# Two of four token blocks through all experts densely, two gathered in one VectorE stream

## The chip, the cores and the metric

One core of one Trainium2 chip runs the kernel. The metric is the device time of one execution in microseconds (us). Everything is float32.

## The reference

A decoder layer on 512 tokens of width 1024. `x = LayerNorm(alpha*x + mixer(x))`, then `out = LayerNorm(alpha*x + PEER(x))`. The mixer is a projection into 3584 columns, four heads of chunked retention and four heads of differential attention, and an output projection. PEER is a retrieval over 16384 experts of one neuron each. Per token and head (8 heads), two query halves are scored against 128 keys each; the best 16 of each half give 256 sums, of which the best 16 name experts, `expert = i*128 + j`, and a softmax over their scores gives the gates. Then

```
u = peer_u[idx]; h = gelu(sum_d x[d] * u[e, d])      # e = 128 picks per token
y = sum_e gate[e] * h[e] * peer_v[idx[e]]
```

One expert row of u or v is 4 KB.

## The kernel before

The program is written engine by engine with semaphores, each engine's instructions in a fixed order. Tokens go in four blocks of 128 (one per partition). Block 0 passes the whole mixer first (`project_0`, `out_0`), gets x1 and its queries, and its experts are then worked on beside the mixer of blocks 1 to 3. Those three share one weight pass (`project_1`), attend one after the other (`attend`, `mixed_out`), get x1 (`ln1(b)`, L1247) and their queries together (`query(1, ...)`, L729). Weights of 2 MB come through two or four slots on SP's queue (`load_w`).

Retrieval of two heads of one block (`retrieve`, L1258) is `best_keys`, `best_pairs` and `best_experts` on VectorE; it writes scores and indices, and ScalarE takes the Exp.

Block 0 gathers u rows and v rows one by one (L438): each indirect DMA brings one row per partition, 0.5 MB, into a ring of 8. VectorE multiplies a u row with x1 and sums it in one instruction (`dots`, L1039; the token block was copied to PSUM). Of the 128 v rows, 32 are scaled and summed on TensorE by diagonal matrices that ScalarE makes from the gates (`diagonals`, `add_rows`, L461), 96 are added into xs on VectorE (`sums`, L1052). `rows(n)` on VectorE takes n groups of four rows and is called in the gaps of the mixer's VectorE work.

Blocks 1 to 3 gather u and v of an expert together (L426), 1 MB per DMA, into 18 slots that cover most of the arena once the mixer is done. VectorE does the dot (L1060), ScalarE the Gelu in groups of four (L971), VectorE the product with the gate (L1067), ScalarE the diagonal (L979), TensorE two matmuls of 512 columns (`add_pairs`, L474). `join_sums` adds the residual and `finish` is the last LayerNorm, then SP stores the block. VectorE's order around all this is its program from L1356 on.

## Time and profile before

| | |
|---|---|
| median of 3 runs | 1658.43 us (1653.55 to 1658.89) |
| span of the profiled execution | 1633.5 us |
| time around the span (median less span) | 24.9 us |
| TensorE, VectorE, ScalarE, GpSimd busy | 78%, 71%, 16%, 38% |
| moved by DMA | 603 MB, mean 369 GB/s |

The profile is of one execution, from its first to its last instruction; the page gives no time of its own for what lies around that, so the runs' median stands beside it. A busy engine is one with an instruction in work, not one at its peak. "PEclk" is the clock granted to TensorE as a share of 2.4 GHz; the DMA share is the mean busy share of sixteen DMA engines, and can read a little above 1. An fp32 matmul appears as two instructions.

### The profile page before, as it was taken

The numbers are of one execution on the slowest core, as the hardware profiler recorded it, in microseconds if no ns is written. First come the engines' busy times: TensorE is split into PE (matmuls) and PEld (weight loads), VectorE is DVE, ScalarE is ACT, GpSimd is POOL, SyncE is SP. The second block draws the span as 40 slices with busy tenths as digits, with TensorE's granted clock in tenths as the row PEclk, the third lists the DMA queues.
The fourth block names the chain that finished last, engine by engine and source line by source line (L and its number), as shares of the span: only waits on it lengthen the run. The fifth ranks groups of instructions, "written<-read, shape, count | busy, mean of one in ns | idle before, by whom it ended". The sixth has DMA issues, their size and how long they took to land.

```text
span 1633.5 us, 11511 instructions
## 1 busy us (share of the span) xinstructions
PE 1276.5 (78%) x3448; PEld 618.1 (38%) x3448; DVE 1155.6 (71%) x2727; ACT 267.2 (16%) x754; POOL 625.2 (38%) x645
## 2 busy tenths in 40 slices
PE   7879979888646994586978687878777878787885
PEld 5465446433323562232323233333333333332332
DVE  1349999767798979987676767776767677764454
ACT  0110000121211111121212121212121212121111
POOL 0004344474445565543434343434342434343320
PEclk9989999999767997798888888989897989899899
DMA  9939798897759898999999999999999999999993
GB/s 339 390 140 353 280 344 312 319 409 274 263 189 335 319 373 329 410 422 421 422 421 421 422 422 421 422 421 422 421 422 421 422 421 422 421 422 421 421 422 127
DMA packets 125710, 603.44 MB, mean 369 GB/s; under 512 B 12624, under 2 KB 14928, under 8 KB 76368
## 3 DMA queue, kind: packets, MB, share of 16 engines
q0 software_dynamic: 92160, 536.91, 81.2%
q1 hardware_dynamic: 33488, 65.80, 11.0%
q8 instruction: 27, 0.44, 0.1%
q14 instruction: 35, 0.29, 0.1%
HBM read 600.57 MB, written 2.10 MB: 369 GB/s over the span
## 4 chain that ended last, share of the span: by engine, by line
DMA 38%; PE 31%; DVE 23%; issue 3%; POOL 2%; SPq 1%; ACT 1%; DVEq 0%; POOLq 0%
DMA arena<-uv,idx 37%; PE W L474 7%; PE W L509 7%; DVE arena L1060 5%; PE ACC L474 4%; DVE xs L1052 4%; PE W L744 3%; PE W L716 3%; PE ACC L461 2%; POOL arena L438 2%; PE W L515 2%; DVE arena L1039 1%; DMA arena<-w_in 1%; DVE cand L1301 1%; DVE cand L1303 1%
## 5 line engine op out<-in xcount | busy, mean ns | idle before, releaser
L474 PE MATMUL W<-arena,fdiag 128*128 128x512 f32 x1024 | 498.9, 648 | 170.1 <-ACT fdiag L979 170.1
L426 POOL DMA_INDIRECT arena<-uv,idx x384 | 367.5, 957 | 586.7 <-PE W L474 355.7
L1060 DVE SCALAR_TENSOR_TENSOR arena<-arena,X 128x1024 f32<-128x1024 f32 x256 | 309.2, 1219 | 200.8 <-DMA arena<-uv,idx 199.7
L438 POOL DMA_INDIRECT arena<-uv,idx x256 | 257.3, 1005 | 372.2 <-DVE idx L1311 125.1
L474 PEld LDWEIGHTS W<-arena,fdiag 128*128 128x128 f32 x1024 | 208.6, 208 | 459.7 <-issue 253.0
L474 PE MATMUL ACC<-arena,fdiag 128*128 128x512 f32 x512 | 254.9, 660 | 69.3 <-ACT fdiag L979 69.3
L1060 DVE SCALAR_TENSOR_TENSOR arena<-arena,W 128x1024 f32<-128x1024 f32 x128 | 154.8, 1219 | 95.8 <-DMA arena<-uv,idx 95.4
L474 PEld LDWEIGHTS ACC<-arena,fdiag 128*128 128x128 f32 x512 | 107.0, 213 | 217.2 <-issue 132.1
L979 ACT ACTIVATE fdiag<-ident,gate 128x128 f32<-128x128 f32 x384 | 123.3, 390 | 354.7 <-DVE gate L1067 351.0
L1039 DVE SCALAR_TENSOR_TENSOR arena<-arena,X 128x1024 f32<-128x1024 f32 x128 | 150.0, 1216 | 24.8 <-DMA arena<-uv,idx 24.3
L509 PE MATMUL W<-arena 128*128 128x512 f32 x320 | 143.7, 605 | 9.7 <-DMA arena<-w_in 9.0
L1052 DVE SCALAR_TENSOR_TENSOR xs<-arena,gate,xs 128x1024 f32<-128x1024 f32 x96 | 123.3, 1284 | 19.3 <-DMA arena<-uv,idx 11.1
L744 PE MATMUL W<-arena 128*128 128x128 f32 (+1 forms) x512 | 116.8, 391 | 1.4 <-ACT arena L912 1.4
L971 ACT ACTIVATE hid<-hid 128x4 f32<-128x4 f32 x96 | 19.7, 205 | 456.5 <-DVE arena L1060 456.5
L744 PEld LDWEIGHTS W<-arena 128*128 128x128 f32 x512 | 80.2, 198 | 36.2 <-ACT arena L912 2.2
L509 PEld LDWEIGHTS W<-arena 128*128 128x128 f32 x320 | 60.8, 194 | 81.9 <-issue 76.9
L515 PE MATMUL W<-arena 128*128 128x128 f32 (+1 forms) x256 | 58.9, 388 | 10.8 <-DVE arena L1157 9.4
L461 PE MATMUL ACC<-arena,fdiag 128*128 128x512 f32 x128 | 59.0, 615 | 4.2 <-DMA arena<-uv,idx 4.2
L515 PEld LDWEIGHTS W<-arena 128*128 128x128 f32 x256 | 39.0, 194 | 28.4 <-issue 11.8
L716 PE MATMUL W<-arena 128*128 128x512 f32 x96 | 43.8, 616 | 0.7 <-ACT arena L912 0.7
L461 PEld LDWEIGHTS ACC<-arena,fdiag 128*128 128x128 f32 x128 | 24.5, 197 | 36.0 <-issue 29.7
L716 PEld LDWEIGHTS W<-arena 128*128 128x128 f32 x96 | 18.7, 198 | 25.1 <-issue 23.2
(178 smaller groups left out, 824.7 us busy)
## 6 DMA issues: line engine op xcount, KB each, us to landing
arena<-w_in SPq DMA_DIRECT2D x13, 2048.0 KB, 13.8
arena<-peer_w_query SPq DMA_DIRECT2D x8, 2048.0 KB, 14.4
arena<-uv,idx POOLq DMA_INDIRECT x640, 25.4
arena<-w_out SPq DMA_DIRECT2D x4, 2048.0 KB, 14.9
arena<-w_in SPq DMA_DIRECT2D x4, 512.0 KB, 6.4
out<-xs SPq DMA_DIRECT2D x4, 512.0 KB, 8.1
arena<-xT SPq DMA_DIRECT2D x1, 1536.0 KB, 18.2
xs<-x SPq DMA_DIRECT2D x1, 1536.0 KB, 17.0
```

Source lines behind the costliest of these rows:

```text
L426: pool.indirect_dma_start(out=fused[slot], out_offset=None, in_=uv, in_offset=bass.IndirectOffsetOnAxis(ap=idx[:, E + n:E + n + 1], axis=0 ...
L438: pool.indirect_dma_start(out=ring[:, r, :], out_offset=None, in_=rows, in_offset=bass.IndirectOffsetOnAxis(ap=idx[:, e:e + 1], axis=0), e ...
L461: last = nc.tensor.matmul(ACC[:, half * HW:(half + 1) * HW], fdiag[:, e % ND, :], ring[:, r, half * HW:(half + 1) * HW], start=e == 0, sto ...
L474: last = nc.tensor.matmul(sum_of(b)[:, half * HW:(half + 1) * HW], fdiag[:, n % ND, :], fused[n % NS][:, D + half * HW:D + (half + 1) * HW ...
L509: last = nc.tensor.matmul(bank, actT[:, k, part * P:(part + 1) * P], wts[slot][:, k, :], start=(k == 0), stop=(k == KD - 1))
L515: last = nc.tensor.matmul(bank[:, at:at + n_tok], wts[slot][:, k, h * P:(h + 1) * P], actT[:, k, toks], start=(k == 0), stop=(k == KD - 1))
L716: last = nc.tensor.matmul(W[:, 2 + half, :], mixT[:, k, :], wts[slot][:, k, :], start=(k == 0), stop=(k == KD - 1))
L744: last = nc.tensor.matmul(dst, wts[slot][:, k, i * P:(i + 1) * P], actT[:, k, toks], start=(k == 0), stop=(k == KD - 1))
L979: nc.scalar.activation(fdiag[:, n % ND, :], ident[:], ACT.Copy, scale=gate[:, E + n:E + n + 1]).then_inc(pair_diag_ready, 1)
L1039: STT(out=ring[:, r, :], in0=ring[:, r, :], scalar=1.0, in1=X[:], op0=ALU.mult, op1=ALU.mult, accum_out=hid[:, e:e + 1]).then_inc(slot_use ...
L1052: STT(out=xs[:, 0, :], in0=ring[:, r, :], scalar=gate[:, e:e + 1], in1=xs[:, 0, :], op0=ALU.mult, op1=ALU.add).then_inc(slot_used[r], 1)
L1060: STT(out=fused[slot][:, 0:D], in0=fused[slot][:, 0:D], scalar=1.0, in1=token_of(b), op0=ALU.mult, op1=ALU.mult, accum_out=hid[:, E + n:E ...
```

## The change

Blocks 1 and 2 (`DENSE`, 256 tokens together) pass through all 16384 experts in 128 tiles of 128 experts. `up(n)` computes the hidden values of tile n, experts on partitions, from a transposed copy of u (`uT`, made on the host like the other layouts); `hidden(n)` takes the Gelu into one of 56 slots; `mask_hidden(n)` multiplies by the gates, which are zero for experts not picked; `add(n, d)` multiplies with 128 rows of v and accumulates in PSUM over all tiles. The gate matrix is made per token from its 128 picks: `hot_quads` writes two one-hot matrices (pick by i, weighted with the gate, and pick by j) for four tokens at a time, `quad` multiplies them on TensorE to 128 x 128 gates, `take_quad` copies those to a stage, and every 32 tokens a stage of 2 MB is written to an array `gd` in device memory. From there `load_g` reads the gates of 8 tiles at a time, 1 MB in pieces of 1 KB.

Blocks 0 and 3 (`GATHERED`) gather in one stream of 512 single rows through the ring of 8, in the order u and v of block 0, u and v of block 3. All dots and all sums are on VectorE; the dot reads x1 in SBUF. `rows(n)` now counts single rows. The diagonals, `add_rows`, `add_pairs` and the copies of x1 to PSUM are gone. GpSimd's first gather waits for all four query products instead of two. Blocks are stored in the order 0, 3, 1, 2.

```diff
+GATHERED = [0, 3]
+DENSE = [1, 2]
+ROWS = 2 * E * len(GATHERED)
+ND = len(DENSE)
+TD = ND * P
+NT = P
+NH = 56
 NS = 18
-EARLY, LATE = 6, 14
-FG = 4
-ND = 6
-QUARTER = E // 4
+UR = 4
+VR = 4
+LEAD = 8
+TAIL = 4
+QUADS = P // 4
+OH_RING = 4
+OH_BANKS = 5
+CHUNK = 32
+NC = TD // CHUNK
+PER_CHUNK = CHUNK // 4
+GT = 8
+UP_FIRST = NH - ND * QUADS // 4
...
+            def load_u(n):
+                if n >= UR:
+                    sp.wait_ge(u_ready, n - UR + 1)
+                elif n < 2:
+                    sp.wait_ge(diff_mixed, NB)
+                else:
+                    sp.wait_ge(mixer_ready, 2 * NB)
+                sp.dma_start(u_ring[n % UR], uT[n].rearrange("p (k e) -> p k e", k=KD)).then_inc(u_landed[n % UR], 16)
+            def load_v(n):
+                if n >= VR:
+                    sp.wait_ge(v_done, n - VR + 1)
+                sp.dma_start(v_ring[n % VR], uv[n * P:(n + 1) * P, D:2 * D]).then_inc(v_landed[n % VR], 16)
+            def load_g(g):
+                if g >= 2:
+                    sp.wait_ge(masked, GT * (g - 1))
+                src = gd[:, :, g * GT:(g + 1) * GT, :].rearrange("c j i t -> j c (i t)")
+                sp.dma_start(g_ring[g % 2], src).then_inc(g_landed[g % 2], 16)
...
+            for i in range(WIN + WOUT + 2):
                 load_w(1, i)
-            sp.wait_ge(x1_ready, NB)
+            for n in range(UR):
+                load_u(n)
+            for i in range(WIN + WOUT + 2, PER_WAVE):
+                load_w(1, i)
+            for n in range(UR, NH + UR):
+                load_u(n)
+            for i in range(2):
+                sp.wait_ge(spill_landed[i], 16 * (NC // 2))
+            load_g(0)
+            for n in range(VR):
+                load_v(n)
+            load_g(1)
+            sp.wait_ge(quad_ready, ND * QUADS)
...
+            for n in range(NT):
+                if n + VR < NT:
+                    load_v(n + VR)
+                if n + NH + UR < NT:
+                    load_u(n + NH + UR)
+                if n % GT == 4 and n // GT + 2 < NT // GT:
+                    load_g(n // GT + 2)
...
+            pool.wait_ge(query_ready, WQ)
+            for s in range(ROWS):
+                g, e = s // (2 * E), s % E
+                col = g * E + e
+                is_u = s // E % 2 == 0
+                if is_u and e % QUARTER == 0:
+                    pool.wait_ge(experts_ready, 4 * GATHERED[g] + e // QUARTER + 1)
+                if s >= RING:
+                    pool.wait_ge(row_used[s % RING], s // RING)
...
+            def up(n):
+                pe.wait_ge(u_landed[n % UR], 16 * (n // UR + 1))
+                if n >= 2:
+                    pe.wait_ge(h_ready, n - 1)
+                for k in range(KD):
+                    last = nc.tensor.matmul(h_bank(n), u_ring[n % UR][:, k, :], actT[:, k, P:P + TD],
+                                            start=(k == 0), stop=(k == KD - 1))
+                last.then_inc(u_ready, 1)
...
+            def quad(q):
+                pe.wait_ge(hot_ready, q + 1)
+                if q >= OH_BANKS:
+                    pe.wait_ge(quad_taken, q - OH_BANKS + 1)
+                bank = quad_bank(q)
+                for m in range(4):
+                    last = nc.tensor.matmul(bank[:, m * P:(m + 1) * P], b_hot[:, q % OH_RING, m, :],
+                                            a_hot[:, q % OH_RING, m, :], start=True, stop=True)
+                last.then_inc(quad_ready, 1)
+            def add(n, d):
+                for half in range(2):
+                    last = nc.tensor.matmul(sum_banks(d)[:, half, :], h_slot(n)[:, d * P:(d + 1) * P],
+                                            v_ring[n % VR][:, half * HW:(half + 1) * HW],
+                                            start=(n == 0), stop=(n == NT - 1))
+                return last
...
+            for b in WAVES[1]:
+                attend(b)
+                mixed_out(b)
             turn_x1(3, out_banks(0))
             query(1, WAVES[1])
-            for b in range(1, NB):
-                add_pairs(b)
+            pe.wait_ge(scores_stored, 4 + 3 * WQ)
+            for n in range(UP_FIRST):
+                up(n)
+            for d in range(ND):
+                turn_picks(d)
+                for q in range(d * QUADS, (d + 1) * QUADS):
+                    quad(q)
+                    if q % 4 == 3:
+                        up(UP_FIRST + q // 4)
+            pe.wait_ge(quad_taken, ND * QUADS)
+            for n in range(NT - TAIL):
+                pe.wait_ge(masked, n + 1)
+                pe.wait_ge(v_landed[n % VR], 16 * (n // VR + 1))
+                for d in range(ND):
+                    last = add(n, d)
+                last.then_inc(v_done, 1)
+                if n + NH < NT:
+                    up(n + NH)
+            pe.wait_ge(masked, NT)
+            for i in range(VR):
+                pe.wait_ge(v_landed[i], 16 * (NT // VR))
+            for d in range(ND):
+                for n in range(NT - TAIL, NT):
+                    last = add(n, d)
+                last.then_inc(acc_ready, 1)
...
+            def hidden(n):
+                act.wait_ge(u_ready, n + 1)
+                if n >= NH:
+                    act.wait_ge(v_done, n - NH + 1)
+                elif n >= 48:
+                    act.wait_ge(experts_ready, 12)
+                elif n >= 40:
+                    act.wait_ge(experts_ready, 8)
+                nc.scalar.activation(h_slot(n), h_bank(n), ACT.Gelu).then_inc(h_ready, 1)
+            def take_picks(d):
+                act.wait_ge(experts_ready, 4 * d + 8)
+                nc.scalar.activation(pk[d % 2][:, 2, :], pk[d % 2][:, 2, :], ACT.Exp).then_inc(pk_exp_ready, 1)
+                act.wait_ge(pk_turned, d + 1)
+                nc.scalar.activation(pT[d % 2], ACC[:, HW:HW + 3 * P].rearrange("p (c t) -> p c t", c=3),
+                                     ACT.Copy).then_inc(pT_ready, 1)
+            def take_quad(q):
+                c, at = divmod(q, PER_CHUNK)
+                act.wait_ge(quad_ready, q + 1)
+                if at == 0 and c >= 2:
+                    act.wait_ge(spill_landed[c % 2], 16 * (c // 2))
+                nc.scalar.activation(stage[c % 2][:, :, 4 * at:4 * at + 4],
+                                     quad_bank(q).rearrange("p (m i) -> p i m", m=4), ACT.Copy).then_inc(quad_taken, 1)
+                if at == PER_CHUNK - 1:
+                    act.wait_ge(quad_taken, q + 1)
+                    nc.scalar.dma_start(gd[c], stage[c % 2]).then_inc(spill_landed[c % 2], 16)
...
+            gate_exp(0)
+            for b in WAVES[1]:
+                attention(b)
+                take_mixed(b)
+                if b > 1:
+                    take_x1(b - 1, out_banks(1))
             take_x1(3, out_banks(0))
...
             query(1, WAVES[1])
...
+            for n in range(UP_FIRST):
+                hidden(n)
+            for d in range(ND):
+                take_picks(d)
+                for q in range(d * QUADS, (d + 1) * QUADS):
+                    take_quad(q)
+                    if q % 4 == 3:
+                        hidden(UP_FIRST + q // 4)
+            gathered_gelu(0)
+            for n in range(NH, NT):
+                hidden(n)
+                if n == NH + 18:
+                    gate_exp(1)
+                elif n == NH + 64:
+                    gathered_gelu(1)
...
+            def norm_picks(d):
+                dve.wait_ge(pk_exp_ready, d + 1)
+                g = pk[d % 2][:, 2, :].rearrange("p (h k) -> p h k", h=PH)
+                link(nc.vector.reduce_sum(gsum[:], g, AX.X))
+                link(nc.vector.reciprocal(gsum[:], gsum[:]))
+                TT(out=g, in0=g, in1=gsum[:].unsqueeze(2).to_broadcast([P, PH, TOPK]),
+                   op=ALU.mult).then_inc(pk_ready, 1)
+            def hot_quads(d):
+                dve.wait_ge(pT_ready, d + 1)
+                for q in range(d * QUADS, (d + 1) * QUADS):
+                    if q >= OH_RING:
+                        dve.wait_ge(quad_ready, q - OH_RING + 1)
+                    for m in range(4):
+                        t = 4 * (q % QUADS) + m
+                        TS(b_hot[:, q % OH_RING, m, :], iota_f[:], pT[d % 2][:, 1, t:t + 1], None, ALU.is_equal)
+                        last = TS(a_hot[:, q % OH_RING, m, :], iota_f[:], pT[d % 2][:, 0, t:t + 1],
+                                  pT[d % 2][:, 2, t:t + 1], ALU.is_equal, ALU.mult)
+                    last.then_inc(hot_ready, 1)
+            def mask_hidden(n):
+                g = n // GT
+                if n % GT == 0:
+                    dve.wait_ge(g_landed[g % 2], 16 * (g // 2 + 1))
+                dve.wait_ge(h_ready, n + 1)
+                h = h_slot(n).rearrange("p (c t) -> p c t", c=NC)
+                TT(out=h, in0=h, in1=g_ring[g % 2][:, :, n % GT * CHUNK:(n % GT + 1) * CHUNK],
+                   op=ALU.mult).then_inc(masked, 1)
...
-                    rows(2)
+                    rows(4)
                     swish_gate(n)
                 else:
-                    rows(1)
+                    rows(2)
...
-            rows(3)
+            rows(8)
             ln1(3)
...
+            rows(12)
+            for s in range(4):
+                retrieve(1, s)
+                rows(3)
+            best_keys(2, 0)
+            norm_picks(0)
+            best_pairs()
+            best_experts(2, 0)
+            hot_quads(0)
+            for s in range(1, 4):
+                retrieve(2, s)
+                rows(3)
+            norm_picks(1)
+            rows(E - taken[0])
+            hot_quads(1)
+            weigh(0)
+            for n in range(LEAD):
+                mask_hidden(n)
+            for n in range(NT):
+                if n + LEAD < NT:
+                    mask_hidden(n + LEAD)
+                if 2 <= n < 14:
+                    s, stage_of = divmod(n - 2, 3)
+                    if stage_of == 0:
+                        best_keys(3, s)
+                    elif stage_of == 1:
                         best_pairs()
...
+                    else:
+                        best_experts(3, s)
+                if taken[0] == 3 * E and n < 66:
+                    pass
+                else:
+                    if n == 66:
+                        weigh(1)
+                    rows(min(4, 3 * E - taken[0]) if n < 66 else 3)
+                if n == 40:
+                    finish(0)
+                elif n == NT - 2:
+                    rows(ROWS - taken[0])
+                    finish(3)
+            for d in range(ND):
+                join_sums(d)
+                finish(DENSE[d])
...
```

## Rows read from the trace of the kernel before

**Rows 1.** Windows: us, busy (instructions) per engine, PEclk, DMA share, GB/s.

```profile
100.00:200.00 100.00, 96.57 (x445) 61.36 (x445) 88.08 (x273) 9.45 (x16) 30.11 (x32) 0.99 0.72 274
200.00:300.00 100.00, 90.37 (x345) 54.68 (x344) 96.94 (x253) 6.81 (x13) 48.73 (x52) 0.97 0.87 329
...
600.00:650.00 50.00, 28.37 (x118) 18.33 (x116) 45.37 (x86) 7.56 (x14) 27.56 (x26) 0.84 0.90 346
...
700.00:800.00 100.00, 78.53 (x159) 32.94 (x158) 75.21 (x184) 17.64 (x53) 38.19 (x40) 0.89 1.01 422
```

**Rows 2.** The page's chain that ended last, by line.

```profile
DMA arena<-uv,idx 37%; PE W L474 7%; PE W L509 7%; DVE arena L1060 5%; PE ACC L474 4%; DVE xs L1052 4%; PE W L744 3%; PE W L716 3%; PE ACC L461 2%; POOL arena L438 2%; PE W L515 2%; DVE arena L1039 1%; DMA arena<-w_in 1%; DVE cand L1301 1%; DVE cand L1303 1%
```

**Rows 3.** The chain in order of time: start us, us, what.

```profile
108.46 7.16 PE W L744 x64
...
172.48 6.87 PE W L509 x16
```

**Rows 4.** Timeline of VectorE, first MAX8 of two retrievals: start, us, what.

```profile
109.13 0.87 DVE L1269 MAX8 best_v<-arena 128x8 f32<-128x128 f32 x4 [14.47 <-ACT arena L935]
...
125.06 0.87 DVE L1269 MAX8 best_v<-arena 128x8 f32<-128x128 f32 x4
```

**Rows 5.** Timeline of VectorE, dots and sums; the landing of gathers, by tile.

```profile
141.06 1.21 DVE L1039 SCALAR_TENSOR_TENSOR arena<-arena,X 128x1024 f32<-128x1024 f32 x1
...
142.19 1.22 DVE L1039 SCALAR_TENSOR_TENSOR arena<-arena,X 128x1024 f32<-128x1024 f32 x1
...
624.83 38.77 DVE L1052 SCALAR_TENSOR_TENSOR xs<-arena,gate,xs 128x1024 f32<-128x1024 f32 x28
...
DMA to landing us min/median/max: 4.1/25.4/34.0
```

**Rows 6.** DMA of 248 to 258, 13 to 60 and 1400 to 1500 us.

```profile
DMA packets 1121, 4.08 MB, mean 408 GB/s; under 512 B 124, under 2 KB 124, under 8 KB 1121
...
DMA packets 9994, 17.29 MB, mean 368 GB/s; under 512 B 1845, under 2 KB 2101, under 8 KB 9992
...
DMA packets 5782, 42.12 MB, mean 421 GB/s; under 512 B 643, under 2 KB 643, under 8 KB 643
```

**Rows 7.** Timeline of TensorE, output of block 3 and queries of blocks 1 to 3.

```profile
503.73 15.82 PE L716 MATMUL W<-arena 128*128 128x512 f32 x32 [0.69 <-ACT arena L912]
...
527.38 1.97 PE L725 MATMUL W<-ident,xs 128*128 128x128 f32 x8 [7.83 <-DVE xs L1112]
530.04 23.22 PE L744 MATMUL W<-arena 128*128 128x384 f32 x64 [0.69 <-ACT arena L912]
553.84 3.00 PE L754 MATMUL W<-arena 128*128 128x128 f32 x24 [0.58 <-ACT arena L929]
...
626.52 3.00 PE L754 MATMUL W<-arena 128*128 128x128 f32 x24 [0.58 <-ACT arena L929]
```

**Rows 8.** Timeline of TensorE, a wait in the projections.

```profile
234.85 6.85 PE L515 MATMUL W<-arena 128*128 128x384 f32 x16 [8.26 <-DVE arena L1157]
```

**Rows 9.** Timeline of VectorE in attention of block 3, a head's first step.

```profile
463.39 0.43 DVE L1203 TENSOR_TENSOR W<-W,mask 128x256 f32<-128x256 f32 x1
...
472.40 0.42 DVE L1203 TENSOR_TENSOR W<-W,mask 128x256 f32<-128x256 f32 x1
```

**Rows 10.** Small VectorE operations: timeline, then a group by form (busy us, mean ns).

```profile
301.33 1.37 DVE L1189 TENSOR_SCALAR arena<-W,mv,rstd 128x128 f32<-128x128 f32 x4
...
498.19 1.13 DVE L1243 SCALAR_TENSOR_TENSOR arena<-W,rstd,arena 128x128 f32<-128x128 f32 x4
...
462.66 0.69 DVE L1092 TENSOR_SCALAR xs<-xs 128x1024 f32<-128x1024 f32 x1
...
L1214 DVE TENSOR_SCALAR arena<-arena,rz 128x256 f32<-128x256 f32 x4 | 1.5, 372 | 0.1
```

**Rows 11.** Timeline of the end.

```profile
1622.73 1.22 DVE L1124 SCALAR_TENSOR_TENSOR xs<-xs,W 128x1024 f32<-128x1024 f32 x1 [7.66 <-PE W L474]
...
1630.49 0.33 SPq L396 DMA_DIRECT2D out<-xs  x1
```

More of the change, by code:

```diff
@@ L400, in _ @@
         def _(pool):
[L401 removed]
+            nc.gpsimd.iota(iota_i[:], pattern=[[1, P]], base=0, channel_multiplier=0).then_inc(iota_ready, 1)
             rows = uv.rearrange("e (c d) -> (e c) d", c=2)
             pool.wait_ge(mixer_ready, 2)
[L404 to L410 removed]
@@ L669, in attend @@
                         score(b, h + 1)
-                    for j in beside[h]:
-                        add_rows(j)
                     n = H * b + h
@@ L882, in attention @@
                     last.then_inc(exps_ready, 1)
-                    for j in beside[h]:
-                        diagonals(j)
-                    if b == 3 and h == 0:
-                        gelu_0(1, 4, 2)
                     act.wait_ge(a_turned, n + 1)
@@ L1042, in sums @@
-            def sums(k):
-                p = AT["V", k]
-                for m, r in enumerate(ring_slots(p)):
-                    e = k * HALF + m
-                    dve.wait_ge(row_landed[r], landed(p))
-                    if e > ON_PE * HALF:
-                        dve.wait_ge(slot_used[slot_of("V", e - 1)[0]], slot_of("V", e - 1)[1])
-                    STT(out=xs[:, 0, :], in0=ring[:, r, :], scalar=gate[:, e:e + 1], in1=xs[:, 0, :],
-                        op0=ALU.mult, op1=ALU.add).then_inc(slot_used[r], 1)
@@ new lines, in mask_hidden, with rows @@
+            def mask_hidden(n):
[6 more added lines that the diff above has]
+                   op=ALU.mult).then_inc(masked, 1)
+            taken = [0]
+            def rows(n):
+                for s in range(taken[0], min(taken[0] + n, ROWS)):
+                    if s // E % 2 == 0:
+                        dot(s)
+                    else:
+                        add_row(s)
+                taken[0] = min(taken[0] + n, ROWS)
@@ L1343, in _ @@
             ln1(0)
-            taken = [0]
-            def rows(n):
-                for k in range(taken[0], taken[0] + n):
-                    if k < HALVES:
-                        dots(k)
-                    else:
-                        sums(k - HALVES + ON_PE)
-                taken[0] += n
             retrieve(0, 0)
```

427 lines of the change are left out of this document (139 added, 288 removed).

## The prediction

> **What bounds the kernel now.** I read the windows table first. Up to 650 us the engines take turns. From 700 to 1600 us the DMA share is 1.01 and the rate 421 to 422 GB/s in each of nine rows of 100 us, of which the first stands; TensorE is busy 79% there and VectorE 75% [rows 1]: this stage, 403 MB of gathered pairs for blocks 1 to 3, is bound by transfers. The chain of waits agrees: 37% of the span is the gather [rows 2]. The change replaces two thirds of that stage, so the question is what the replacement is bound by, and when it can begin. The span is 1633.5 us; the median of the runs, 1658.4, lies 24.9 above it. I work in span and add 24.9.
>
> **Prices.** A TensorE instruction of 512 columns costs 429 ns (6.87/16), one of 128 columns 112 ns (7.16/64) [rows 3]; every fp32 matmul is two of them. So 256 columns cost 215 ns, half of 512, and `up` (8 matmuls, 256 columns) is 3.44 us, `add` for both blocks (4 matmuls, 512 columns) 3.43 us. These are prices at the clock of 1.00; waits bring the granted clock to 0.89 from 700 us on [rows 1]. A retrieval is 15.9 us from its first MAX8 to the next one's [rows 4]. A dot is 1.145 us apart [rows 5] with one operand in PSUM; a sum, with both in SBUF and a wait for the sum before, is 1.385 us (38.77/28) [rows 5]. The new dot has both in SBUF and no such wait: between these, and I take 1.21. Transfers: where only 4 KB packets of gathered rows run, 408 GB/s at a full share; 2 KB packets 368; 8 KB pairs 421 [rows 6]. One 0.524 MB transfer of 4 KB pieces is thus 1.285 us of all sixteen engines.
>
> **Up to x1 of block 3.** ln1(3) ends at 527.3 [rows 7]. Before it VectorE now takes 24+7+30+8 = 69 rows where it took 156. To 312 us TensorE is nearly the bound (97% and 90% busy [rows 1]); of its waits on VectorE, 8.3 us before L515 [rows 8], some 8 go. In attention a head's cycle was 9.0 us in block 3, with four sums (5.5) in it [rows 9], and longer in block 1, where `add_rows` had 16 more TensorE instructions per head. With two dots it is 9.0-5.5+2.4 = 6 us in block 3, and 5 in block 1, whose rows of 256 keys are half as long. Followed through, with two out_halves at 14 us (32 instructions) and ln1 at 8 us unchanged: block 1's output ends near 346 instead of 382, block 2's near 397 instead of 454, ln1(3) at 461. TensorE, no longer kept busy by `add_rows`, drops to the lower clock more often (the output took 15.8 us behind a pause [rows 7], 13.7 at 429 ns); 5 us for that: 466. Bounds 450 and 490. Gain 61 us.
>
> **Queries to the first dense add.** The query stage took 102 us from ln1's end to the last key scores (527.4 to 629.5) [rows 7]: it ends at 568. TensorE then does 40 `up`s, 138 us, to 706. And here VectorE stands: after retrieve(1,0..3) and best_keys(2,0) it does norm_picks(0), which waits for the Exp of take_picks(0), and ScalarE has that behind hidden(39) in its program. VectorE gets there near 592 (in the trace the first scores came 28 us after ln1, the next ones every 24.2 [rows 7]; so 494, 518, 543 and 567, the last followed by 15.9, three dots at 1.21 and 5.3 of best_keys) and stands until 708, 116 us, with the rows, the retrievals and the one-hot matrices queued behind it. DMA meanwhile has only the u tiles, 0.524 MB per 3.44 us.
> Then in VectorE's order: norm, pairs and experts 11.6 (720); hot_quads(0); 3 retrievals and 9 dots, 59; norm_picks(1) 2.5; 26 dots, 33 at the gather's pace; hot_quads(1). A one-hot pair is two TENSOR_SCALARs of 128 elements, one with one scalar read from SBUF and one with two. The trace has the second kind from PSUM at 1.37 us for four, 0.32 apart, and a STT of that size at 0.26 apart; the first kind takes 0.37 alone at 256 elements [rows 10]. Bounds: 0.32 and 0.32 from above; 0.16 and 0.16 from below (half the time of 256 elements, less the overlap of 0.08 by which a dot's 1.22 us stand 1.145 apart). I take 0.21+0.27 = 0.48 us per token, nearest the SBUF row and the STT: 62 us per block (41 to 82). TensorE needs only 4*2*0.112 = 0.9 us per quad and 0.86 for its share of an `up`, so VectorE sets the pace: end of hot_quads(1) at 938.
> The VectorE page of the Trainium skill ("VectorE: DVE Perf Modes", "The perf-mode tier table") says that an fp32 tensor_scalar within SBUF runs at two elements a cycle. The immediate-scalar row (1024 elements in 0.69 us [rows 10]) agrees, the row with a scalar from SBUF (256 in 0.37 us) speaks for less. By the page, as an estimate, a pair would cost 0.3 us, TensorE would set the pace at 56 us per block and some 12 us would go.
> A quad's copy on ScalarE is 512 columns and hidden in VectorE's 2 us. Last taken quad, a 2 MB spill (about 8 us), a 1 MB load of gates (5), mask: the first add is at 954. Nothing hides this chain; it is all on the path. Bounds 905 and 1000.
>
> **Edits at nothing.** GpSimd now waits for the fourth query product instead of the second; that is done when the last L744 group of block 0 ends, near 134, and VectorE wants the first row at 141 [rows 5]: covered, since a row lands in 4.1 us at the least [rows 5], and 3 us if not. Moved and shared buffers (gn, lam_in, the longer iota) change no count. SP's loop asks for v, then u, then gates, each behind a wait for TensorE; v is asked for three tiles ahead, about 24 us, against 25 us from a gather's issue to its landing under full load [rows 5]: equal, so it may cost, and that is in rival C. ScalarE loses 416 diagonals and gains 128 Gelus and 64 copies: it bounds nothing.
>
> **The dense loop.** What is left at 954: 384 rows (201 MB), v 67 MB, 68 u tiles (36 MB), gates 17 MB: 321 MB. TensorE alone would need 128*3.43+72*3.44 = 687 us; 321 MB at 408 GB/s is 787. VectorE's sum is 128*1.21+256*1.385+120 masks*0.42 [rows 9]+64 retrieval+16 = 640. Transfers bound it. Gate packets are 1 KB, smaller than any here in number; at the 2 KB rate 0.131 MB is 0.36 us, at half of it 0.72, at none 0. Tile by tile:
> n=0, 1: 12 us. n=2 to 13: VectorE is late, 4*1.385+0.42+5.3 = 11.3 us each, 135; TensorE uses up the lead of 8 tiles, 55 us, just here. n=14 to 63: four rows, u, v, gates: 6*1.285+0.36 = 8.07 us each, 404, less 10 for the full ring; above TensorE's 6.87/0.9 = 7.6, hence no second cost. n=64, 65: 3. n=66 to 108: three rows and v, 4*1.285+0.36 = 5.5 each, 236 less 10; TensorE 3.43 to 4.3, VectorE 4.6. The last 11 tiles on TensorE at 3.6: 40. With 3 for the first masks the sum is 813: last acc_ready at 1768 (954+813, rounded up). The end: joining and finishing block 1 overlaps the last 6.9 us of block 2's adds, block 2 costs 9; before, 8 us lay between the last matmul's end and the store's issue and 3 behind it [rows 11]. +14: span 1782, time 1807.
> The rate of 4 KB pieces on two queues at once is in no row; the 4 KB and 8 KB rates bound it above: 408 to 422, 787 or 760 us. The DMA page of the Trainium skill ("DMA: Bandwidth & Descriptors", "Where 436 GB/s comes from") puts the ceiling of the sixteen ports at 435 GB/s; no row here is above 422 over 10 us or more. As an estimate by the page, 321 MB would be 738 us, still above TensorE's 687.
>
> **Rivals.**
> A, faster: TensorE is the bound from the queries' end on, and never waits. 568 + 56*3.44 + 57 (quads) + 687 = 1505, +14+24.9 = 1544. For it: TensorE's work is large and the ring of 56 hidden tiles is there to decouple. Against: VectorE's wait behind hidden(39), and 321 MB in 687 us are 467 GB/s. It decides when TensorE's waits from the queries' end to the last add sum to under 114 us (1658-1544); I count 263 (1768-1505). Chance 0.04.
> B: the loop goes at TensorE's pace (transfers keep up because buffers are full and the share is better than I think), with the start at 954: 954+687+10+14+24.9 = 1690. Against: the rate. Chance 0.06.
> C: the start is right and the loop worse: the two queues and the in-order VectorE leave gaps, so that full share is not held (from 600 to 650 us, with rows alone, the share was 0.90 and the rate 346 [rows 1]): 321 MB at 370 is 868, +81: 1888. For it: rows are asked for in bursts of four and the ring holds 8, gates are small packets. Against: u and v rings fill in. Chance 0.16.
> D: VectorE passes norm_picks(0) early (ScalarE's order is as I read it, so this needs short `up`s): the start comes 60 us or more earlier, 1740. Chance 0.04.
>
> **How the numbers follow.** The forecast has 0.68, A 0.04, B 0.06, C 0.16, D 0.04, and 0.02 is for a sum of gains that ends level. Faster or slower begins at 0.3%, 5 us, which is about what a measurement of this kernel can tell from none. Slower 0.94, same 0.02, faster 0.04. Range: forecast -50 (start at 905 or 422 GB/s, not both) to +70 (start at 990, or half of C): 1745 to 1880.
>
> **What would show it.** Chain of waits and timeline: VectorE idle for some 115 us before the first reduction of norm_picks, released by ScalarE's Exp; hot_quads 62 us per block; first add near 954. Windows: DMA share near 1.0 and about 400 GB/s from some 150 us into the loop, TensorE at about 85% and then 65%. ln1(3) near 466. It is wrong if the loop's DMA share stays below 0.9 with TensorE above 95% busy (B), if VectorE does not stand before norm_picks(0) (D), or if the loop shows gaps in all engines (C).

## The result and the profile after

The changed kernel takes 1803.4 us (median of 4 runs, 1801.6 to 1806.4), the kernel before, measured beside it, 1658.7 (4 runs, 1653.6 to 1663.1): a ratio of 1.088, 95% interval 1.085 to 1.090. 1807 was forecast. In all later comparisons, on one chip, the kernel before took 1637.4 to 1637.7 and the changed one 1802.2 (1800.8 to 1805.7, 5 runs), ratio 1.101 (1.099 to 1.103). Differences between experiments are taken there.

Windows of the changed kernel, first coarse, then closer. Columns: us, busy (instructions) of TensorE, its weight loads, VectorE, ScalarE and GpSimd, granted clock, DMA share, GB/s.

```profile
0.00:600.00 600.00, 502.48 (x1929) 308.44 (x1930) 372.90 (x1120) 80.48 (x203) 130.22 (x106) 0.90 0.58 204
600.00:949.00 349.00, 229.35 (x1270) 206.18 (x1269) 215.92 (x805) 63.56 (x121) 42.96 (x35) 0.83 0.51 179
949.00:1741.00 792.00, 682.08 (x2079) 404.31 (x2080) 589.57 (x900) 30.44 (x76) 425.65 (x376) 0.93 1.01 393
1741.00:1801.00 60.00, 43.86 (x98) 18.75 (x96) 22.68 (x61) 0.00 (x0) 0.00 (x0) 0.92 0.33 114
...
600.00:650.00 50.00, 50.00 (x233) 44.01 (x233) 0.00 (x0) 5.75 (x15) 0.00 (x0) 1.00 0.46 150
...
969.00:1101.50 132.50, 132.50 (x464) 87.93 (x463) 125.82 (x308) 10.04 (x22) 60.24 (x49) 1.00 0.98 368
1101.50:1497.00 395.50, 335.66 (x1099) 212.56 (x1097) 270.37 (x399) 17.49 (x47) 218.44 (x200) 0.93 1.03 404
1497.00:1740.00 243.00, 193.14 (x461) 91.61 (x462) 179.78 (x178) 2.14 (x6) 139.13 (x123) 0.91 1.02 398
```

The same first stretches of the kernel before, and its last one once more without its end:

```profile
0.00:600.00 600.00, 494.35 (x1796) 284.17 (x1797) 444.37 (x1051) 86.69 (x226) 234.25 (x239) 0.91 0.83 307
600.00:949.00 349.00, 252.44 (x576) 112.89 (x575) 268.04 (x633) 60.28 (x171) 151.03 (x155) 0.86 1.00 409
949.00:1633.50 684.50, 529.72 (x1080) 221.05 (x1078) 443.16 (x1045) 120.26 (x357) 239.88 (x253) 0.90 0.97 404
...
949.00:1600.00 651.00, 510.37 (x1037) 213.23 (x1036) 428.37 (x1013) 117.30 (x347) 239.88 (x253) 0.90 1.01 422
```

Rate times length gives the bytes. Before, 184 and 143 MB were carried by 949 us and 277 MB behind it. After, it is 122 and 62 MB, then 311 MB to 1741 us and 7 at the end. The change carries 100 MB less (603 against 503 MB), but 142 MB less of it in the first 949 us. So 41 MB more are left for the stage in which transfers are the bound in both kernels.

From 949 us on the kernel before takes 684.5 us and the changed one 852, and this is the whole difference of the spans, 167.5 us. It splits by the same windows. Before, the rate of 422 GB/s is held for 651 us, and 33.5 us follow in which little is moved. After, 311 MB take 792 us at 393 GB/s, and 60 us follow. At 422 GB/s the 311 MB would take 737 us. So 86 us of the loss are the bytes left over (737 less 651), 55 us are the lower rate (792 less 737), and 26 us are the longer end, in which TensorE finishes its last tiles. Half of the loss is thus time before 949 us in which the DMA engines had little to do. The window from 600 to 650 us shows this at its purest: TensorE never pauses, VectorE does nothing, and the DMA share is 0.46, where it was 0.90 [rows 1].

VectorE's longest wait (line waited for: us in total, times, longest), its one-hot pairs, and TensorE at the marks that the prediction set:

```profile
DVE gsum L1317 <- ACT both_uses L980: 118.3, 1, 118.3
```

```profile
720.24 0.28 DVE L1330 TENSOR_SCALAR arena<-iota_f,both_uses 128x128 f32<-128x128 f32 x1
720.43 0.34 DVE L1331 TENSOR_SCALAR lng<-iota_f,both_uses 128x128 f32<-128x128 f32 x1
720.69 0.28 DVE L1330 TENSOR_SCALAR arena<-iota_f,both_uses 128x128 f32<-128x128 f32 x1
```

```profile
465.61 1.97 PE L697 MATMUL W<-ident,xs 128*128 128x128 f32 x8 [7.83 <-DVE xs L1103]
...
564.96 3.00 PE L726 MATMUL W<-arena 128*128 128x128 f32 x24 [0.58 <-ACT arena L943]
568.65 3.72 PE L736 MATMUL X<-arena 128*128 128x256 f32 x16 [0.69 <-ACT dkT L949]
...
710.10 0.55 PE L746 MATMUL ACC<-ident,both_uses 128*128 128x128 f32 x3 [3.05 <-DVE both_uses L1319]
...
949.22 4.61 PE L763 MATMUL W<-arena 128*128 128x512 f32 x5 [11.53 <-DMA arena<-uv]
```

L697 is the transposes of x1 of block 3 (before: 527.4 [rows 7]), L736 `up`, L746 the transposes of the picks, L763 `add`. Of the chain of waits, the way of the gates and the end, in order of time (start us, us, what):

```profile
934.90 7.15 DMA gd<-arena
944.79 12.63 DMA arena<-gd
...
1710.77 18.58 DMA arena<-uv
1729.49 39.72 PE W L763 x88
1769.22 4.36 DMA arena<-uv
1773.71 8.82 PE W L763 x16
1782.56 1.23 DVE xs L1110
```

The first request for gates, the first mask, and VectorE at four marks of the loop. L1342 is `mask_hidden`; iteration n of VectorE's loop begins with the mask of tile n+8, so the rows stand for iterations 2, 14, 64 to 66 and 109:

```profile
942.13 0.38 SPq L369 DMA_DIRECT2D arena<-gd  x1
...
947.89 1.43 DVE L1342 TENSOR_TENSOR arena<-arena 128x256 f32<-128x256 f32 x4 [9.17 <-DMA arena<-gd]
...
968.86 0.42 DVE L1342 TENSOR_TENSOR arena<-arena 128x256 f32<-128x256 f32 x1
...
1101.53 0.42 DVE L1342 TENSOR_TENSOR arena<-arena 128x256 f32<-128x256 f32 x1
...
1496.26 1.08 DVE L1342 TENSOR_TENSOR arena<-arena 128x256 f32<-128x256 f32 x3
...
1739.77 3.77 DVE L1342 TENSOR_TENSOR arena<-arena 128x256 f32<-128x256 f32 x11
```

TensorE's waits in the loop, 1000 to 1801 us:

```profile
PE W L763 <- DMA arena<-uv: 67.4, 12, 11.1
PE X L736 <- ACT arena L975: 26.3, 1, 26.3
```

### The profile page after: what moved, and what is told of

Same layout as the page of the kernel before. It is cut to its first block, busy times and chain, and to the rows that moved or that the text cites. A ratio compares the mean times of both kernels' runs of the same rounds, so it can differ in the third digit from the quotient of the medians.

```text
span 1801.0 us, 15732 instructions
## 1 busy us (share of the span) xinstructions
PE 1457.8 (81%) x5374; PEld 937.7 (52%) x5374; DVE 1201.1 (67%) x2884; ACT 174.5 (10%) x400; POOL 598.8 (33%) x517
## 4 chain that ended last, share of the span: by engine, by line
PE 35%; DVE 24%; DMA 24%; POOL 7%; issue 6%; SPq 1%; ACT 1%; DVEq 0%; POOLq 0%
DMA arena<-uv,idx 21%; PE X L736 9%; POOL arena L443 7%; PE W L716 6%; PE W L483 6%; DVE xs L1070 5%; DVE arena L1052 3%; PE W L763 3%; PE W L688 2%; PE W L489 2%; DVE lng L1331 2%; PE W L756 1%; DVE arena L1330 1%; DMA arena<-uv 1%; DMA arena<-w_in 1%
## 5 line engine op out<-in xcount | busy, mean ns | idle before, releaser
L736 PE MATMUL X<-arena 128*128 128x256 f32 x2048 | 458.6, 380 | 27.0 <-ACT arena L975 26.3
L736 PEld LDWEIGHTS X<-arena 128*128 128x128 f32 x2048 | 389.1, 191 | 111.6 <-issue 61.9
L763 PE MATMUL W<-arena 128*128 128x512 f32 x768 | 363.2, 625 | 62.9 <-DMA arena<-uv 52.8
L1070 DVE SCALAR_TENSOR_TENSOR xs<-arena,gate,xs 128x1024 f32<-128x1024 f32 x256 | 328.7, 1284 | 110.9 <-DMA arena<-uv,idx 98.3
L1052 DVE SCALAR_TENSOR_TENSOR arena<-arena,xs 128x1024 f32<-128x1024 f32 x256 | 306.7, 1223 | 95.5 <-DMA arena<-uv,idx 92.7
L763 PEld LDWEIGHTS W<-arena 128*128 128x128 f32 x768 | 152.6, 201 | 240.8 <-issue 205.1
L483 PE MATMUL W<-arena 128*128 128x512 f32 x320 | 143.7, 605 | 9.6 <-DMA arena<-w_in 8.9
L1331 DVE TENSOR_SCALAR lng<-iota_f,both_uses 128x128 f32<-128x128 f32 x256 | 106.6, 431 | 0.0
L483 PEld LDWEIGHTS W<-arena 128*128 128x128 f32 x320 | 60.8, 194 | 81.7 <-issue 77.0
L716 PEld LDWEIGHTS W<-arena 128*128 128x128 f32 x512 | 80.4, 199 | 36.3 <-issue 2.4
L1330 DVE TENSOR_SCALAR arena<-iota_f,both_uses 128x128 f32<-128x128 f32 x256 | 94.5, 370 | 0.0
L763 PE MATMUL W<-arena,kT 128*128 128x512 f32 x128 | 63.1, 644 | 21.7 <-DMA arena<-uv 14.2
L1317 DVE TENSOR_REDUCE gsum<-both_uses 128x8 f32<-128x128 f32 x2 | 0.6, 284 | 118.3 <-ACT both_uses L980 118.3
L763 PE MATMUL W<-arena,rv 128*128 128x512 f32 x128 | 58.4, 608 | 14.8 <-DMA arena<-uv 11.9
L763 PEld LDWEIGHTS W<-arena,kT 128*128 128x128 f32 x128 | 25.8, 206 | 54.6 <-issue 39.5
L489 PEld LDWEIGHTS W<-arena 128*128 128x128 f32 x256 | 39.1, 194 | 22.8 <-issue 6.3
```

Of the source, the lines that this page charges most:

```text
L483: last = nc.tensor.matmul(bank, actT[:, k, part * P:(part + 1) * P], wts[slot][:, k, :], start=(k == 0), stop=(k == KD - 1))
L489: last = nc.tensor.matmul(bank[:, at:at + n_tok], wts[slot][:, k, h * P:(h + 1) * P], actT[:, k, toks], start=(k == 0), stop=(k == KD - 1))
L716: last = nc.tensor.matmul(dst, wts[slot][:, k, i * P:(i + 1) * P], actT[:, k, toks], start=(k == 0), stop=(k == KD - 1))
L736: last = nc.tensor.matmul(h_bank(n), u_ring[n % UR][:, k, :], actT[:, k, P:P + TD], start=(k == 0), stop=(k == KD - 1))
L763: last = nc.tensor.matmul(sum_banks(d)[:, half, :], h_slot(n)[:, d * P:(d + 1) * P], v_ring[n % VR][:, half * HW:(half + 1) * HW], start=( ...
L1052: STT(out=ring[:, r, :], in0=ring[:, r, :], scalar=1.0, in1=xs[:, GATHERED[g], :], op0=ALU.mult, op1=ALU.mult, accum_out=hid[:, col:col + ...
```

## The experiments

Three theories were carried. F is the forecast's: the start is late because VectorE stands behind ScalarE's order, and transfers bound the loop. Its rivals said that TensorE sets the loop (B), or that the loop's queues leave gaps (C). In the expectations T stands for B's claim, or for the bound that it names; the other letters are explained where they stand. The forecast had come out near the measured time, so each experiment takes one step of it away, to see whether the step costs what it was priced at.

**The changed kernel again, unchanged.**

> The changed kernel as it is, on the chip of this call, so that the other kernels of the call have it beside them: 1800 to 1806 us by every theory.

1802.2 us. The baseline of the differences below.

**1. The picks of the first dense block earlier** (TensorE and ScalarE alike).

```diff
+def tiles_first():
+    for n in range(8):
+        yield "tile", n
+    yield "picks", 0
+    for q in range(QUADS):
+        yield "quad", q
+        if q % 4 == 3:
+            yield "tile", 8 + q // 4
+    for n in range(16, 40):
+        yield "tile", n
+    yield "picks", 1
+    for q in range(QUADS):
+        yield "quad", QUADS + q
+        if q % 2:
+            yield "tile", 40 + q // 2
...
-            for n in range(UP_FIRST):
-                hidden(n)
...
+            for what, n in tiles_first():
+                {"tile": hidden, "picks": take_picks, "quad": take_quad}[what](n)
```

> The changed kernel (1803 us) with take_picks(0), turn_picks(0) and the quads of block 1 put behind 8 tiles of up and hidden instead of 40; 8 tiles go beside those quads, 24 behind them, 16 beside the quads of block 2. Theory F (the stand of VectorE before norm_picks(0), 118 us in the trace, is on the path, and the dense loop is bound by transfers and only moves): the stand falls under 15 us. VectorE's chain would put the end of hot_quads(1) near 808, TensorE's, with 2.6 us per quad there, near 829; the first add comes near 843 instead of 949, the span ends some 100 to 106 us earlier: 1697 to 1703. Rival S (the stand is covered: TensorE's tiles before the loop, or the transfers in it, would take the gain): 1785 or more.

Measured 1749.1 us (1746.3 to 1751.6), 53 less. The first add and VectorE's wait:

```profile
894.84 3.75 PE L781 MATMUL W<-arena 128*128 128x512 f32 x4 [11.40 <-DMA arena<-uv]
```

```profile
DVE gsum L1323 <- ACT both_uses L992: 40.7, 2, 32.9
```

The start came 54.4 us earlier and the time fell by 53: what comes off the start comes off the time. norm_picks(0) itself began 113.7 us earlier (595.5 us against 709.2). Two things took half of that back before the first add. The same stand returned, 32.9 us long, before norm_picks(1), as that Exp now lay behind 24 tiles in ScalarE's program. And hot_quads(1) took 77 us (795.5 to 872.4) instead of 58, beside 16 `up`s where 8 had been; 2.4 us per quad, near the 2.6 that the expectation had for TensorE. The stand was moved in part, not removed.

**2. Block 0's rows taken in VectorE's stand**, with the Gelu that releases its sums at tile 18.

```diff
             best_keys(2, 0)
+            rows(E - taken[0])
+            weigh(0)
+            rows(40)
             norm_picks(0)
...
-            rows(E - taken[0])
             hot_quads(1)
-            weigh(0)
```

> The changed kernel with the stand kept but filled: the last 26 dots of block 0, weigh(0) and 40 of its sums run before norm_picks(0), and gathered_gelu(0) moves behind hidden(18). Theory F: the 26 dots leave the path ahead of hot_quads(1), -33 to -41 us at the first add (908 to 916 instead of 949), and 40 rows fewer are left for a loop bound by transfers, 40 x 1.29 = 51 us: 1803 - 84 to 92, so 1711 to 1719; if u tiles and rows together (152 GB/s and more) pass 408 GB/s, the 40 sums last 80 us instead of 55 and still end before 708. Rival T (the loop is bound by TensorE): only the 33 to 41 us, 1762 to 1770. Rival S: no more than 15 us in all.

Measured 1739.4 us (1735.7 to 1743.6), 63 less. From 600 to 700 us, and the first add:

```profile
600.00:700.00 100.00, 86.73 (x396) 75.85 (x395) 67.04 (x84) 9.68 (x26) 60.41 (x57) 0.93 1.02 405
```

```profile
931.32 2.04 PE L763 MATMUL W<-arena 128*128 128x512 f32 x2 [11.65 <-DMA arena<-uv]
```

The stand can carry transfers at full rate, and what it carries comes off the end: 18 us from the earlier start, the other 45 from a loop that is 40 rows shorter (40 at 1.285 are 51). The start gained 18 and not 33 to 41, because rows and u tiles together took until 727 us where VectorE had been released at 709.

**3. Block 3's gathered experts left out** (256 of the 512 rows; that block gets no expert part). The loop's other work is unchanged.

```diff
-ROWS = 2 * E * len(GATHERED)
+ROWS = 2 * E
```

> The changed kernel without block 3's 256 gathered rows (134 MB left out of the loop, with their dots, sums and weights; the expert part of block 3 is left out of the output). Theory F: the loop is at TensorE's pace once the rows of block 0 are in (tile 32), and ends near 702 to 710 us behind its start instead of 833: span about 1675, time 1670 to 1685. Rival T (TensorE already bounds the loop): 1790 to 1805, as TensorE's work is unchanged. Rival G (the rate falls whenever both queues run, with or without block 3's rows): 1720 to 1760.

Measured 1676.3 us (1674.2 to 1680.7), 126 less. The windows once the rows are done:

```profile
1250.00:1600.00 350.00, 350.00 (x1063) 201.78 (x1062) 26.57 (x78) 12.12 (x32) 0.00 (x0) 1.00 0.52 174
```

134 MB out of 503 bring 126 us where they would take 329 at 408 GB/s: TensorE, busy 100% for 350 us, is the second bound, and it stands 126 us behind the first.

**4. Half of the adds left out**: block 2's adds of tiles 1 to 119, so that its result is incomplete.

```diff
-                for d in range(ND):
+                for d in range(1 if n else ND):
                     last = add(n, d)
```

> The changed kernel with 119 of 128 pairs of add matmuls of block 2 left out (its expert part is left out of the output; all transfers, masks, dots and sums stay): 205 us of TensorE work less, nearly all of it in the loop. Theory F: the loop stays bound by transfers until the last row, and only the tiles behind it gain, about 11 x 1.7 = 19 us, and some 10 at the start, where TensorE was busy all the time from 950 to 1100: 1770 to 1795. Rival T: 1600 to 1640.

Measured 1789.2 us (1784.5 to 1791.2), 13 less.

```profile
949.00:1750.00 801.00, 544.59 (x1643) 335.35 (x1644) 596.82 (x926) 30.52 (x76) 423.79 (x376) 0.84 1.01 393
```

Over the same stretch the unchanged kernel, in the run taken as baseline, reads:

```profile
949.00:1750.00 801.00, 686.18 (x2094) 406.71 (x2095) 596.76 (x926) 30.51 (x76) 426.65 (x376) 0.94 1.01 392
```

TensorE's busy time there fell by 142 us (at a granted clock of 0.84 instead of 0.94), and the DMA share and rate did not move. So TensorE does not set this loop, and B falls.

**5 and 6. The two waits that nobody had foreseen.** In experiment 5 the gates, behind which SP's v tiles queue, are asked for later; in experiment 6 the Gelu of block 3 comes last in ScalarE's program, so that it no longer holds `hidden` back.

```diff
-                if n % GT == 4 and n // GT + 2 < NT // GT:
+                if n % GT == 7 and n // GT + 2 < NT // GT:
```

> The changed kernel with load_g asked for at n%8 = 7 instead of 4. In the trace SP stands at load_g(15) for the mask of tile 111 while four v tiles wait behind it, and TensorE waits 11 us for v at 1718 to 1729 (67 us in all from 1000 us on, in 12 waits). Theory F (only the last of these waits is not covered by the transfers that bound the loop): 8 to 15 us faster than e7, about 1790. Rival V (v waits cost all along): 40 us or more faster. Rival N (the transfer rate sets all, the last wait too): within 3 us of e7.

```diff
-                elif n == NH + 64:
+                elif n == NT - 1:
                     gathered_gelu(1)
```

> The changed kernel with gathered_gelu(1) behind the last hidden tile instead of hidden(120). In the trace ScalarE stands in it for 49 us until block 3's last dot, and TensorE's up waits 26 us for ScalarE at 1471 to 1497, with DMA at its full share meanwhile. Theory F (transfers bound the loop): within 4 us of e7. Rival T (TensorE's 26 us are on the path): 15 to 26 us faster.

Measured 1802.5 (1799.6 to 1806.6) and 1802.1 us (1800.0 to 1804.6): nothing, both. TensorE's waits in the loop with the gates later,

```profile
PE W L763 <- DVE arena L1342: 30.5, 24, 3.6
PE X L736 <- ACT arena L975: 30.3, 1, 30.3
PE W L763 <- DMA arena<-uv: 27.8, 4, 8.4
```

show that the wait for v (67.4 before) fell to 27.8 and came back as a wait for masks. Where transfers are the bound, TensorE's waits only change their name. F's own 8 to 15 us for the gates were wrong.

**7. Balanced.** Both dense blocks' picks early (tiles 7 and 28), only 40 tiles ahead, four rows where two stood, rows in every gap of attention and in those of block 1's retrieval, none in block 2's, the Gelu of block 0 before the queries and that of block 3 behind tile 102, gates as in experiment 5.

```diff
+AHEAD = 40
...
+    for n in range(7):
+        yield "tile", n
+    yield "picks", 0
...
+    for n in range(15, 28):
+        yield "tile", n
+    yield "picks", 1
...
                 if FILLS[n][1] == RG:
-                    rows(4)
+                    rows(8 if i == 6 else 4)
...
                     if b > 1 and h == 0:
+                        rows(6)
                         ln1(b - 1)
-                rows(2)
+                rows(3)
                 diff_norm(b)
...
-            rows(12)
+            rows(14)
             for s in range(4):
                 retrieve(1, s)
-                rows(3)
+                if s < 3:
+                    rows(5)
```

> A version made from the findings: early picks as in e1 with the second pick also ahead of most tiles (7 tiles, quads of block 1 with 8, 13 tiles, quads of block 2 with 8, 4 tiles; up runs 40 tiles ahead instead of 56), more rows in the gaps in which VectorE waits before the queries and between retrievals (148 by then plus a few instead of 102, all dots of block 0 among them, weigh(0) before the queries), none between the retrievals of block 2, gates asked for as in e5, gathered_gelu(1) behind hidden(102). Theory F: end of hot_quads(1) near 765, first add near 785, 357 rows (187 MB) and 315 MB in all left for the loop, 778 us at 405 GB/s: the adds end near 1580, the span near 1600, 1595 to 1625 us, faster than the kernel before (1638 and 1659 in two calls). Rival T (TensorE's 742 us with the waits it meets at the lower clock bound it): 1640 to 1680. Rival P (rows in the gaps delay the queries, weights behind them on the DMA engines): ln1(3) and the queries slip by more than 15 us, 1640 or more.

Measured 1652.9 us (1650.7 to 1654.7), 149 less than the changed kernel, ratio to the kernel before 1.009 (1.008 to 1.011). Its windows:

```profile
0.00:200.00 200.00, 175.05 (x769) 107.93 (x770) 117.42 (x359) 22.30 (x55) 39.46 (x35) 0.97 0.80 293
200.00:820.00 620.00, 517.88 (x2222) 367.93 (x2221) 513.77 (x1605) 116.12 (x254) 177.02 (x138) 0.88 0.63 221
820.00:1600.00 780.00, 718.82 (x2313) 441.67 (x2312) 555.99 (x886) 36.29 (x91) 398.29 (x346) 0.97 1.00 387
...
900.00:1000.00 100.00, 99.56 (x351) 66.23 (x349) 85.21 (x148) 5.75 (x15) 54.14 (x46) 1.00 0.99 375
...
1400.00:1500.00 100.00, 100.00 (x309) 58.36 (x308) 59.70 (x58) 3.83 (x10) 53.13 (x44) 1.00 0.98 381
```

The first add is at 804.5 us, 145 earlier, and nearly all of the gain of 149 is that. The time lies 28 us above F's range (1595 to 1625) and inside T's (1640 to 1680). Two things are in the miss. Transfers at a share of 1.00 moved 387 GB/s over 780 us, not the 406 of the stretch from 1200 to 1400 us after, worth 780*19/406 = 36 us; and from 1300 to 1500 us, as from 850 to 1000, TensorE is busy 99% or more. The start was expected near 785 us and came some 20 later. Half of this is once more an order of requests:

```profile
781.59 14.14 SPq L379 DMA_DIRECT2D arena<-uT  x5
795.85 0.38 SPq L392 DMA_DIRECT2D arena<-gd  x1
...
802.46 2.77 DVE L1353 TENSOR_TENSOR arena<-arena 128x256 f32<-128x256 f32 x8 [25.57 <-DMA arena<-gd]
```

The last spill landed at 785.9 us (asked for at 778.8, 7.1 us on its way), but SP asked for the gates only at 795.9, since loads of u tiles that wait for TensorE's `up`s stand before them in its program. No run took these 10 us away.

**8 and 9. Sixteen rows in the last gap**, where VectorE of the balanced kernel waits 33 us for the gates (25.57 and 7.45); and, on top, the gates asked for at iteration 2 of a group of eight.

```diff
             hot_quads(1)
+            rows(16)
             for n in range(LEAD):
```

> The balanced version, and 16 of block 0's rows taken by VectorE behind the second block's one-hot matrices, before the first mask; there VectorE stood 25.6 and 7.5 us for the gates' way through DRAM with the DMA share at 0.65. Theory T (transfers are the bound from 820 us on, so what is carried before that comes off the end): 16 rows at 1.285 us each are 20.6 us; the first add stays at 804, 1652.9 becomes 1630 to 1640, at or just below the kernel before on this chip (1637). Rival P (TensorE's work is by now the bound: 1446 us busy, share 0.88): the time stays within 5 us of 1653. Rival Q: the rows' transfers delay the spill and the gates, the first add slips by 10 us and only half is left: 1642 to 1648.

> The same with the gates of each group of eight tiles asked for at its iteration 2 and not 7; in the balanced version VectorE stood 88.4 us in six places for them, 15.1 of it after 1450 us. Theory T (the transfers' rate, 387 GB/s at a share of 1.00, sets all): VectorE's stands go, the time stays within 4 us of the version with the rows alone. Rival V: VectorE's lateness leaves TensorE waiting for masks (39.9 us) and the rows late at the end: 15 to 30 us less, 1605 to 1625.

Measured 1662.2 us (1660.1 to 1665.7) and 1665.3 (1661.1 to 1668.8): 9 and 12 slower than the balanced kernel. Experiment 8 lies outside all three of its ranges; 9 stays within the 4 us of it that T gave. Three rows bear on why the 16 rows brought nothing: TensorE's first add of experiment 8 (804.5 in 7), VectorE's first mask, and a window:

```profile
L786 PE MATMUL W<-arena x24: 592/592/1191, 816.8 to 836.3; 128*128 128x512 f32 x24
```

```profile
814.09 2.77 DVE L1353 TENSOR_TENSOR arena<-arena 128x256 f32<-128x256 f32 x8 [9.76 <-DMA arena<-gd]
```

```profile
1300.00:1400.00 100.00, 100.00 (x346) 65.57 (x346) 52.26 (x56) 5.97 (x16) 41.52 (x36) 1.00 0.88 329
```

The spill was not delayed (it landed at 786.2 us, 785.9 in 7), and the gates were asked for at the same time (795.5, 795.9 in 7). But beside the rows' transfers they took 18.6 us to land instead of 6.6, and the first add came 12.3 us later. This is Q's mechanism, with another end: from the first add to the end of the span the kernel needed 841.2 us where the balanced one needed 846.4, so 5 us came off for 16 rows and not the 20.6 of their transfers. In that stretch TensorE, at 100% busy from 1300 to 1400 us, let the DMA share fall to 0.88 (1.00 and 386 GB/s in 7). So in the balanced kernel both bounds seem to take turns, and rows moved earlier no longer come off the end one to one; no run took TensorE's work out of it to show this. V's 15 to 30 us for the gates did not come. That experiment 9 is another 3 us slower than 8 is no price of the gates: the intervals overlap (1.0138 to 1.0179 and 1.0138 to 1.0185), and in its profiled execution VectorE is already 5 us later at norm_picks(0) (601.0 against 595.9), before the edit can act. None of these kernels beats the one before.

## Why the prediction was right, and where it was not

**Up to x1 of block 3.** 466 forecast, 465.6 measured. This agrees better than its parts do: block 1's output ends at 353.2 us (338.14+15.04, L688) where 346 was forecast, block 2's at 405.3 (391.14+14.15) where 397 was. The 8 us were made up in block 3, which took 60 us instead of 69. That the sum hits is in part luck.

**VectorE's stand.** Forecast 116 us before norm_picks(0), behind hidden(39): measured 118.3. Experiment 1 shows that what its edit took from the start comes off the time, 53 us for 54.4; that the whole stand would is not shown, since the edit took only part of it away. Rival D falls. A falls by its own test: TensorE stood 235 us from 568 to 1783 us (busy 980 of 1215), where 263 were counted and under 114 would have spoken for A. No mean over the page gives the stand: it came from reading two engines' programs side by side, one waiting for the other's later instruction.

**One-hot pairs.** 0.48 us taken, 0.45 measured (720.24 to 720.69): 0.19 to the second instruction, 0.26 to the next pair. The bounds of 0.32 and 0.16 per instruction held it. The VectorE page's two elements a cycle ("VectorE: DVE Perf Modes", "The perf-mode tier table", the Trainium skill) gave 0.3 for a pair as an estimate; for 128 elements with scalars read from SBUF the trace disagrees, 0.45. Its table is for 2048 elements, 1227 ns, which scale to 0.15 for a pair; where the rest of the 0.3 came from the prediction does not say.

**Queries, `up`s, and the chain to the first add.** Queries end at 568.0 (568 forecast), the 40 `up`s at 707.1 (706), the first add comes at 949.2 (954). The 5 us lie before the end of hot_quads(1): 933 where 938 was forecast. Pairs were 4 us a block cheaper, and the 26 dots before them dearer, 39 us (835.7 to 875.0) where 33 were taken. The gates' way behind it was right, 16 us: the first load of gates was asked for at 942.1 and let the first mask begin at 947.9, 5.8 us later (5 forecast). The second, 12.6 us to land beside four v tiles, is not waited for by the first add.

**The loop.** The tile count of the forecast can be laid beside VectorE's marks:

| part | forecast, us | measured, us |
|---|---|---|
| first add to iteration 2 | 15 | 19.6 |
| iterations 2 to 13 | 135 | 132.7 |
| iterations 14 to 65 | 397 | 395.4 |
| iterations 66 to 108 | 226 | 242.9 |
| from there to the end of the adds | 40 | 42.8 |
| sum | 813 | 833.4 |

So the slow tiles, late on VectorE, were priced rightly, and so were the 52 tiles behind them, with the "less 10 for the full ring" in their 397. That TensorE uses up its lead of 8 tiles in them is there too: it is busy 132.5 of 132.5 us, and pauses soon after. The step that was wrong is the term for n=66 to 108, 17 of the 20 us. It was 43 tiles at 5.5 us, 236, and "less 10" a second time. Measured are 5.65 us per tile and no such gain: the stretch moved 243*398/1000 = 96.7 MB, which at the priced 408 GB/s are 237 us. So 10 us are the ring's allowance, taken twice, and 6 the rate of 398. Between 1101.5 and 1497 us the rate is 404, within 1% of the price. C's mechanism, a share that is not held, is not there: after the first 20 us (0.90) the share is 0.97 or more in every 50 us until the rows are done. Why the rate is only 368 GB/s at a share of 0.98 from 969 to 1101.5 us is open. Experiment 4 rules B out; experiment 3 shows TensorE within 126 us of being the bound.

**Waits that the sum leaves out:** the Gelu of block 3 on ScalarE, 26.3 us of TensorE's time, which the prediction does not name, and v behind other requests on SP's queue, part of 67.4 us, which it left to rival C. Experiments 5 and 6 price both at nothing here.

**The end.** 14 us forecast from the last acc_ready, 18.4 measured (1782.6 to 1801.0).

**The time around the span.** Here the prediction was wrong, and luck saved it: its other errors went the other way. It added 24.9 us, the median of the runs less the profiled span. After the change span and time lie 2.1 apart (1801.0; that run took 1803.1), and in every execution that has both, of either kernel, between 1.7 and 2.2. Before's span of 1633.5 fits the 1637.4 it shows in the later comparisons, not the 1658.4 of the first runs: the difference was between executions and not a cost around each. So the span was forecast at 1782 and came out at 1801, 19 low (the start 5 early, the loop 20 and the end 4 longer); the addition was 23 high; together 4 high. On one chip the loss is 165 us and not 145; 149 were forecast. Why the kernel before shows 1637 in one place and 1658 in another, when the changed one shows 1802 and 1803, is not settled; no run tested it.

## What to carry to other kernels

When transfers bound the last stage, count the bytes that each stage carries before it: replacing 268 MB of pairs by 168 MB of tiles and gates was lost here, for half of the loss because the stages in front carried 142 MB less, and for a third because what was left moved at 393 GB/s and not at 422. A total that comes out right says little of its terms: lay each term beside its mark in the trace, since two of them here had errors of 17 and 23 us in opposite directions. When one engine's result is needed by another early, look for where the first engine's program puts it, not for when its inputs are ready; and when one such stand is removed, look for the next one behind it. A wait that a trace names on an engine that is not the bound may be worth nothing (experiments 5 and 6), and an engine that is busy 86% of the bound's stage (686 of 801 us) is the next bound once that stage shrinks (experiment 3).

## What the hardware showed that was not expected

Gathered rows and plain loads on two queues at once, 4 KB pieces but for the gates' 1 KB, reach 406 GB/s (1200 to 1400 us), within 1% of one queue alone at 408 [rows 6]. The ceiling of 435 GB/s that the Trainium skill gives ("DMA: Bandwidth & Descriptors", "Where 436 GB/s comes from") is not reached by any window here; 8 KB pairs came nearest, 421 to 422. Pieces of 4 KB instead of 8 KB went with 4% less of the rate at the same full share.

A dot with both operands in SBUF runs 1.15 us apart, no dearer than from PSUM (1.145 [rows 5]); 1.21 was taken.
